# The front of a three-layer network: modulation sums by tile pairs and as row sums on VectorE, projections and block attention moved beside the recurrence

## The reference

```python
mod = (jax.nn.silu(c) @ w_ada[l] + b_ada[l])[:, None, :]        # 1024 -> 6144
sh1, sc1, gt1, sh2, sc2, gt2 = jnp.split(mod, 6, axis=-1)
xn = rms_norm(h, norm1_g[l]) * (1.0 + sc1) + sh1
proj = xn @ w_in[l]
qm, km, vm, zrw, gate_logits = jnp.split(proj, split_at, axis=-1)
qm = rope_partial(rms_norm(qm.reshape(B, S, 8, 64), q_norm_g[l]), positions)
km = rope_partial(rms_norm(km.reshape(B, S, 8, 64), k_norm_g[l]), positions)
o_moba = moba_attention(qm, km, vm)                             # causal, one block of 256
zrw = token_shift(zrw, rwkv_mu[l])
o_rwkv = rwkv7_time_mix(zr, zk, zv, zw, za, zg, ...)            # scan over 256 tokens, 8 heads of 64
g_moba, g_rwkv = jnp.split(jax.nn.sigmoid(gate_logits), 2, axis=-1)
mixed = g_moba * (o_moba @ w_proj_moba[l]) + g_rwkv * (o_rwkv @ w_proj_rwkv[l])
h = h + gt1 * (mixed @ w_out[l])
xn2 = rms_norm(h, norm2_g[l]) * (1.0 + sc2) + sh2
```

## Time and profile before

| | |
|---|---|
| median of 3 runs | 1921.0 us |
| the profiled execution | 1917.7 us, span 1915.9 us |
| PE busy | 1781.4 us (93%) |
| DVE, ACT, POOL busy | 1144.5, 793.8, 206.1 us |
| first matmul | at 16.09 us |
| first matmul of a projection | at 47.81 us |
| first matmul of `wq`, where the part that the change touches ends | at 437.83 us |
| PE busy before and after that point | 367.6 and 1413.8 us |

### The profile page before, as it was taken

One profiled execution on the slowest core, in us unless ns is written; L12 is line 12 of the kernel. 1 busy time (PEld: TensorE's weight loads), 2 busy tenths in 40 slices (PEclk: granted clock), 3 DMA queues, 4 the chain that ended last, 5 costly groups with the idle time before them and its releaser, 6 DMA issues.

```text
span 1915.9 us, 30068 instructions
## 1 busy us (share of the span) xinstructions
PE 1781.4 (93%) x13092; PEld 1631.8 (85%) x13092; DVE 1144.5 (60%) x1707; ACT 793.8 (41%) x1143; POOL 206.1 (11%) x84
## 2 busy tenths in 40 slices
PE   4979898888989899999999999999999998999987
PEld 2778787788989899998898888888899997988887
DVE  2373239555588748875435998555664546454654
ACT  3533323634434432234443222444434545544543
POOL 0030134200556620000000000000000000000000
PEclk8899999998999999999999999999999998999999
DMA  8223712243435443335453333555654343433320
GB/s 314 76 109 141 256 68 89 100 160 137 164 145 179 173 146 119 111 110 198 176 186 144 118 125 110 197 193 189 238 178 157 128 165 114 153 132 131 110 89 23
DMA packets 40022, 280.29 MB, mean 146 GB/s; under 512 B 4433, under 2 KB 4689, under 8 KB 7506
## 3 DMA queue, kind: packets, MB, share of 16 engines
q1 hardware_dynamic: 39024, 275.53, 40.4%
q10 hardware_dynamic: 866, 2.84, 0.4%
HBM read 277.30 MB, written 1.05 MB: 145 GB/s over the span
## 4 chain that ended last, share of the span: by engine, by line
PE 78%; DVE 13%; ACT 5%; POOL 2%; DMA 2%; issue 1%; ACTq 0%; DVEq 0%
PE ps L481 77%; DVE WL L1629 2%; POOL WL L2310 2%; ACT ar L1092 2%; DVE ar L1621 2%; ACT WH L1100 1%; DVE ar L1602 1%; DVE ar L2026 1%; DVE ar L2023 1%; DVE ar L1613 1%; DMA con<-in_con 1%; DVE ar L2030 1%; PE ps L609 0%; DVE ar L2042 0%; DMA ar<-in_in_qk 0%
## 5 line engine op out<-in xcount | busy, mean ns | idle before, releaser
L481 PE MATMUL ps<-RH,WH 128*128 128x256 f32 x2520 | 744.3, 295 | 52.8 <-DVE RL L1661 13.3
L481 PE MATMUL ps<-RL,WH 128*128 128x256 f32 x2520 | 722.8, 287 | 0.0
L481 PE MATMUL ps<-RH,WL 128*128 128x256 f32 x2520 | 721.9, 286 | 0.0
L1629 DVE TENSOR_TENSOR WL<-ar,WH 128x1024 fp32r<-128x1024 f32 (+1 forms) x398 | 468.2, 1208 | 374.2 <-ACT WH L1100 374.1
L1100 ACT ACTIVATE WH<-ar 128x1024 fp32r<-128x1024 f32 (+1 forms) x478 | 480.0, 1039 | 283.3 <-PE ps L481 269.1
L481 PEld LDWEIGHTS ps<-RH,WH 128*128 128x128 f32 x2520 | 493.8, 196 | 71.1 <-issue 21.5
L481 PEld LDWEIGHTS ps<-RL,WH 128*128 128x128 f32 x2520 | 494.2, 196 | 3.4 <-issue 2.9
L481 PEld LDWEIGHTS ps<-RH,WL 128*128 128x128 f32 x2520 | 493.3, 196 | 0.0
L481 PE MATMUL ps<-ar 128*128 128x64 f32 (+9 forms) x2988 | 339.4, 300 | 32.6 <-DMA con<-in_con 16.1
L481 PEld LDWEIGHTS ps<-ar 128*128 128x128 f32 (+6 forms) x2988 | 281.2, 172 | 71.2 <-issue 23.4
L481 PE MATMUL ps<-WH,RH 128*128 128x512 f32 (+1 forms) x704 | 261.8, 372 | 6.3 <-DVE RL L2004 6.3
(11 more groups left out here) (134 smaller groups left out, 979.9 us busy)
## 6 DMA issues: line engine op xcount, KB each, us to landing
ar<-in_u SPq DMA_DIRECT2D x64, 1024.0 KB, 4.8
ar<-in_v SPq DMA_DIRECT2D x64, 1024.0 KB, 4.7
ar<-in_ada SPq DMA_DIRECT2D x24, 1024.0 KB, 5.1
ar<-in_in_g SPq DMA_DIRECT2D x8, 1024.0 KB, 4.7
ar<-in_wq SPq DMA_DIRECT2D x8, 1024.0 KB, 4.8
ar<-in_a_qk SPq DMA_DIRECT2D x8, 1024.0 KB, 10.6
ar<-in_a_v SPq DMA_DIRECT2D x8, 1024.0 KB, 4.8
ar<-in_a_g SPq DMA_DIRECT2D x8, 1024.0 KB, 4.7
```

Of the source, the lines that this page charges most:

```text
L481: ins = q.matmul(o, l, r, start=start and i == 0, stop=stop and i == len(pairs) - 1, skip_group_check=skip)
L1629: q.tensor_tensor(l[:, x:z, :], src[:, x:z, :], h[:, x:z, :].bitcast(F32), ALU.subtract).then_inc(*v.up(("lo", n, i)))
```

## The change

It rewrites the order of the front and four of its parts.

1. **First modulation by tile pairs.** Chunk j of `ada` (j = 0 to 7) now holds scale and shift of feature tile j, and its sum follows its own product. DVE makes the two columns of `mod` for tile j, XM for it and, one tile later, the rest in RL; ACT makes RH tile by tile. Chunk 7 comes after the first half of `in_wag`. Of the constants only 134 columns (ones, selector, eps) are loaded at the start; the other 1664 and the small LoRA weights are issued by SP before the second `in_rkv` chunk. The rotary angles move behind the first projection.
2. **The other 4096 modulation sums as row sums.** Chunks `adr` hold 2 x 128 columns of `w_ada` transposed, 1024 long; c comes once more, as 128 equal rows (`cwide`), and DVE makes one sum by a `scalar_tensor_tensor` with `accum_out`, 32 in all, at places given by `DOTS`. PE, ACT and PSUM have no part in it.
3. **Projections.** `in_qk` stands beside the first solve (two units a step), the first half of `in_g` beside the second, the rest beside `states` (`UNITS`). The key norm and rotary steps stand beside the second solve (`queries`); the query norm is no longer applied to the queries but as a row factor of the scores (`q_rms`).
4. **Block attention** runs beside `states`, three sub-steps after each of its first 11 half steps (`HEADS`). The output norm of the recurrence is done by token halves; its second half stands beside `pm`, which now comes before `pr`. X is given up to the queries and keys and loaded again before `wo`.
5. The ring has six banks beside the recurrence, not five; the turns of v, al, be and kd and the bonus product move behind the start of `in_v`.

```diff
 WEIGHTS = {
-    "ada": (8, 2, 24), ...
+    "ada": (8, 2, 8), "adr": (2, 8, 16), ...
+DOTS = ((1, 1, 1, 1, 1, 1, 1, 1, 2, 2, 2, 2), (0, 0, 1, 1, 1, 1, 1, 1, 1, 1, 0, 0),
+        (0, 1, 0, 1, 0, 1, 0, 1, 0, 1, 0, 1, 0, 1, 0, 1))
+UNITS = ((2,) * 12, (1,) * 8 + (2,) * 4, (1, 0) * 5 + (1,) + (2,) * 5)
+HEADS = (3,) * 11 + (0,) * 5
...
@@ tensor_program: ada
-    def ada(j, more, of=ring):
+    def ada(j):
...
         ins.then_inc(*p.up(("ada", j)))
-        if more:
-            ada_sum(j - 1)
+        p.wait_ge(*on(("out", ("ada", j))))
+        b = bank(("ada sum", j))
+        for f in range(2):
+            ins = mm(b[:, f:f + 1], [(m.ada_rows[j % 2][:, f * P:(f + 1) * P], cst("sel"))])
+        ins.then_inc(*p.up(("ada sum", j)))
@@ tensor_program: front
-        for j in range(4):
-            ada(j, j > 0)
+        ada(0)
+        ada(1)
         colsum(("norm1",), m.XN, 8, "x squared")
-        for j in range(4, 8):
-            ada(j, True)
-        ada_sum(7)
+        for j in range(2, 7):
+            ada(j)
         zs = chain(proj_steps("in_wag", 0, by="xs"), proj_steps("in_rkv", 0, js=KRV))
-        some(zs, 8)
+        some(zs, 2)
+        ada(7)
+        some(zs, 6)
...
-        fill = beside_recurrence()
-        some(fill, 3)
         for hf in range(2):
-            for _ in pair(hf):
-                some(fill)
-        finish(fill)
-        more = proj_steps("in_qk", 0, of=side)
-        for _ in states():
-            some(more)
-        finish(more)
-        gates = proj_steps("in_g", 0, of=side)
-        for _ in norms():
-            some(gates, 4)
+            for i, _ in enumerate(pair(hf)):
+                some(dots, DOTS[hf][i])
+                some(fill, UNITS[hf][i])
+                if (hf, i) == (1, 0):
+                    q_sums()
+                    blksum("k norm", m.squares[1], ("qk squared", 1))
+                if hf == 1 and 5 <= i < 9:
+                    partners(2 * i - 10)
...
-        for i, _ in enumerate(at):
-            some(gates, i % 3 < 2)
+        for i, _ in enumerate(states()):
+            some(dots, DOTS[2][i])
+            some(fill, UNITS[2][i])
+            some(at, HEADS[i])
+            if i == 9:
+                y_sum("y mean", 0, m.Yy, ("out", ("y", 1)))
+            if i == 11:
+                y_sum("y var", 0, m.Ysq, ("y squared", 0))
+        steps = proj_steps("pm", 8, "oms")
+        some(steps, 2)
+        y_sum("y mean", 1, m.Yy, ("out", ("y", 3)))
+        some(steps, 5)
+        y_sum("y var", 1, m.Ysq, ("y squared", 1))
+        finish(steps)
         proj("pr", 12, "ors")
@@ vector_program
+    def dot_chunks():
+        for j in range(16):
+            feed.take()
+            ...
+            v.wait_ge(*m.loaded(c))
+            for f in range(2):
+                x, i = w[:, 1024 * f:1024 * f + 1024], 16 + 2 * j + f
+                v.wait_ge(*on("c wide silu"))
+                q.scalar_tensor_tensor(x, x, 1.0, m.cwide, ALU.mult, ALU.mult,
+                                       accum_out=mod[:, i:i + 1]).then_inc(*v.up(("adr", j)))
+                yield
@@ sync_program
+        if c == CHUNKS.index(("in_rkv", KRV[1])):
+            for dst, src in ((m.con[:, C1A:], m.D["con"][:, C1A:]), (m.lw[:, 0:512], m.D["w2a2"]), (m.lw[:, 512:1024], m.D["g2"]),
+                             (m.posi.bitcast(I32), m.D["pos"]), (m.w0[0:1, :], m.D["w0row"])):
+                q.dma_start(dst, src).then_inc(m.lora_loads, 16)
```

More of the change, by code:

```diff
@@ L43 @@
 WEIGHTS = {
-    "ada": (8, 2, 24), "in_wag": (8, 2, 1), "in_rkv": (8, 2, 6), "in_v": (8, 2, 2), "in_qk": (8, 2, 4),
+    "ada": (8, 2, 8), "adr": (2, 8, 16), "in_wag": (8, 2, 1), "in_rkv": (8, 2, 6), "in_v": (8, 2, 2), "in_qk": (8, 2, 4),
     "in_g": (8, 2, 8), "pm": (4, 4, 2), "pr": (4, 4, 2), "wo": (8, 2, 4), "wq": (8, 2, 8), "sub": (1, 16, 1),
@@ L50 @@
 }
-RAW = ("ada", "sub")
+RAW = ("ada", "adr", "sub")
 KRV = (2, 3, 0, 1, 4, 5)
@@ L877, in beside_recurrence @@
         yield from tok_steps("in_v", 0, of=side)
+        turn("v", m.zv, ("z", 12), side)
+        yield
         for nm, src in (("al", m.al), ("be", m.be), ("kd", m.kd)):
-            turn(nm, src, "al be", side)
+            turn(nm, src, "rwkv in", side)
             yield
-        for j in range(8, 24):
-            ada(j, j > 8, side)
+        yield from proj_steps("in_qk", 0, of=side)
+        yield from proj_steps("in_g", 0, of=side)
+    def dot_chunks():
+        for _ in range(16):
+            feed.take()
             yield
-        ada_sum(23)
+            yield
     def up(b_):
@@ L1203, in front @@
         AC(m.XN, m.X, ACT.Square, "x squared")
-        for j in range(4):
-            feed.take()
+        for j in range(2):
             ada_rows(j)
@@ L1299, in half_tanh @@
-        def half_tanh(t, f, n):
-            a.wait_ge(*on(t))
-            q.activation((m.Gm if f < 8 else m.Gr)[:, f % 8:f % 8 + n, :], pairs(tile(t)), ACT.Tanh,
-                         scale=0.5).then_inc(*a.up(("out", t)))
-        gates = walk("in_g", feed, half_tanh)
-        for _ in norms():
-            some(gates, 4)
+        a.wait_ge(*on("angle cos"))
+        AC(m.cA, m.cA, ACT.Sin, "rope ready")
+        a.wait_ge(m.c_load, 16)
+        AC(m.c_sigmoid, m.cwide, ACT.Sigmoid, "c wide sigmoid")
@@ new lines, in front @@
+        fill, dots = beside_recurrence(), dot_chunks()
+        some(fill, 4)
+        for hf in range(2):
+            for i, _ in enumerate(zip(group(2 * hf), group(2 * hf + 1))):
+                some(dots, DOTS[hf][i])
+                some(fill, UNITS[hf][i])
+                if (hf, i) == (0, 11):
+                    for k in range(4):
+                        AC(m.Aa[:, k, :], m.Aa[:, k, :], ACT.Identity, "bonus and shift", bias=vc("ln_b", k))
+                if (hf, i) == (1, 0):
+                    a.wait_ge(*on("q sums"))
+                    AC(m.q_rms, tile("q sums")[:, 0:16], ACT.Sqrt, ("out", "q sums"), bias=cst("eps", 3, 4))
+                    for f in range(2):
+                        t = ("k norm", f)
+                        a.wait_ge(*on(t))
+                        AC(half_of(m.k_root, 2 * f), tile(t), ACT.Sqrt, ("out", t), scale=1.0 / 64, bias=cst("eps", 0, 1))
@@ new lines, in queries @@
+    def queries(i):
+        if 2 <= i < 6:
+            k, r = m.qk[:, i + 2, :], m.k_root[:, i - 2, :]
+            v.wait_ge(*on(("out", ("k norm", 1))))
+            REC(r, r)
+            v.wait_ge(*on(("out", ("in_qk", 6))))
+            TT(k, k, r, ALU.mult, "k scaled")
+        if i == 2:
+            v.wait_ge(*on(("out", "q sums")))
+            REC(m.q_rms, m.q_rms)
+        if 6 <= i < 10:
+            f = 2 * i - 12
+            o, t = m.qk[:, f:f + 2, :], ("rotA", f)
+            r = m.rot[:, f % 4:f % 4 + 2, :]
+            v.wait_ge(*on("rope ready"))
+            v.wait_ge(*on(t))
+            TT(r, pairs(tile(t)), bc(m.sA, 2), ALU.mult, ("out", t))
+            TT(o, o, bc(m.cA, 2), ALU.mult)
+            TT(o, o, r, ALU.add, "qk ready")
@@ new lines, in scaled_scores, with y_centred, y_scaled @@
+    def scaled_scores(h, s, b):
+        for tt, (x, z) in enumerate(((0, 128), (128, 384))):
+            STT(s[:, x:z], b[:, x:z], m.q_rms[:, 8 * tt + h:8 * tt + h + 1], cst("mask3", x, z), ALU.mult, ALU.add)
+    def y_centred(hf):
+        y, t = m.Yy[:, :, hf * P:hf * P + P], ("y mean", hf)
+        v.wait_ge(*on(t))
+        STT(y, b4(tile(t)), -1.0 / 64, y, ALU.mult, ALU.add, ("y centred", hf))
+        v.mark(("out", t))
+    def y_scaled(hf):
+        ts = slice(hf * P, hf * P + P)
+        y, r = m.Yy[:, :, ts], m.Yrt[:, :, ts]
+        v.wait_ge(*on(("out", ("y var", hf))))
+        REC(r, r)
+        v.wait_ge(*v.last())
+        for k in range(4):
+            q.scalar_tensor_tensor(y[:, k, :], y[:, k, :], vc("ln_g", k), r[:, k, :], ALU.mult, ALU.mult).then_inc(*v.up())
+        v.wait_ge(*on("bonus and shift"))
+        TT(y, y, m.Aa[:, :, ts], ALU.add)
+        TT(y, y, m.Gg[:, :, ts], ALU.mult)
```

458 lines of the change are left out of this document (235 added, 223 removed).

## The result

The changed kernel takes 1963.9 us (median of 4 runs), the kernel before 1921.1 (4 runs): a ratio of 1.021, 95% interval 1.019 to 1.024. It is slower by 43 us; the forecast was 32 us faster. The first matmul of `wq` comes at 483.6 us in place of 437.8. From there on nothing has moved: 1478.8 us against the last row. So the loss lies in the front.

What follows compares the result with a forecast made beforehand. PE work was taken to bound the kernel, PE being busy for 93% of the span. Stages of 55.2 + 64.6 + 135.5 + 98.7 + 51.9 made a front of 405.9 against 437.8 us, so 1921.0 - 31.9 = 1889; range 1862 to 1912.

Steps and rivals of the forecast that it cites:

- rival D: Row sums on DVE: each takes two passes, 2.3 us in place of 1.23; 1905 us in all; chance 0.08.
- The second solve: Second solve: 28.8 us of solve, 23.0 of `in_g`, 7.8 of sums and rotary products, late first chunk 2.5; 62.3 us.
- the tail: `pr` to the end of the front: 51.9 us for 63.3 before, since `pm` has moved ahead; bounds 51 and 56.
- a sign that its terms are wrong: Front: PE busy for over 370 us would show the terms wrong; about 339 was expected.
- 1. Start, to the LoRA products: Start of the kernel to the LoRA products: 55.2 us for 60.8 before; bounds 50 and 62.
- the `ada` round of 2.4 us: Start: one `ada` chunk needs product, row copy 0.4, sum and signals, 2.4 us together.
- 2. To the first mask: LoRA products to the solve's first quads: 64.6 us for 68.1 before, bounds 59 and 70; first mask near 121.
- Rival B: DVE and POOL block each other: a full half lost for 12 chunks, 29 us; 1918, no change; chance 0.10.
- 3. The first solve: First solve: 58.9 us of PE work plus standstills of 6.2, 3.7, 1.2 and 3.2 us; 73.2 us.
- rival C: Three load slots: each of 12 weight chunks beside solves and states holds PE up 5.1 us; 1936; chance 0.10.
- 4. Solves to `pr`: End of the solves to `pr`: 98.7 us for 148.0 before, 75 to the last y, then 23.7; bounds 88 and 118.
- an unchanged idle time of 70: Front: PE work falls from 367.6 to about 339 us; with idle time unchanged the front takes 409 us.

Runs made afterwards that it cites:

- The filling: Changed kernel plus ten more 128 x 512 matmuls at the start, between an `ada` product and its sum: 1956.4 us.
- without the chunks: Changed kernel without its sixteen row-sum chunks, neither their loads nor their sums: 1927.2 us, ratio 1.0045.
- With the filling in place: Changed kernel plus two more 128 x 512 matmuls ahead of the three transposes of each head, 16 in all: 1949.9 us.
- short sums: Kernel before with `ada` chunks 8 to 23 as row-sum chunks on VectorE, each sum over 8 columns of 1024: 1900.4 us, ratio 0.989.
- the kernel with row sums alone: Kernel before with only `ada` chunks 8 to 23 made sixteen row-sum chunks on VectorE, at the same places: 1924.0 us, ratio 1.0015.

## Why the prediction was wrong

**Held.** A row sum in the changed kernel:

```profile
139.13 1.22 DVE L1945 SCALAR_TENSOR_TENSOR ar<-ar 128x1024 f32<-128x1024 f32 x1
140.27 0.08 DVE L1945 DVE_READ_ACCUMULATOR ar<-ar 128x1 f32 x1
```

It takes 1.22 us, what follows starts 1.15 us behind its start, and the read of the accumulator adds 0.08, so 1.24 was right and rival D false. The rule of the Trainium skill that stood behind rival D ("Vector Engine (DVE) Microarchitecture Reference", "Points that are easy to get wrong") does not hold here: the form takes 1.22 us with the accumulator and 1.23 without it. The second solve took 61.3 us for 62.3, the tail 53.0 for 51.9. The first PE instruction, at 8.8 for 7.5, was nearly right.

**The whole.** The front is 77.7 us over its forecast. Of this 39.5 are PE's busy time (378.5 for 339) and 38 its idle time (105 for 67). The prediction had named the first as a sign that its terms are wrong (over 370), and it gave slower than before a chance of 0.10.

**1. Start, to the LoRA products: forecast 55.2, measured 63.6.** The term that failed is the `ada` round of 2.4 us: 3.4 at the lower clock, for three chunks. I had it in the bounds ("with products and sums twice as long") and left it out of the value, though the trace of the kernel before has such products too:

```profile
35.56 1.93 PE L481 MATMUL ps<-ar 128*32 128x256 f32 x16
```

The filling brings the 2.4 us back. The column sum took 2.8 us more than forecast, 6.46, and with filling ahead of it is back at 3.70, though the windows give the granted clock as 1.00 around it (18 to 26 us). X landed 2.6 us late, at 13.7.

**2. To the first mask.** The stage took 72.5 us, I had 65.8. The four `rk` products stand beside POOL:

```profile
112.88 3.94 DVE L1828 SCALAR_TENSOR_TENSOR ar<-ar,vec 128x256 f32<-128x256 f32 x4
...
124.31 5.72 DVE L1838 SCALAR_TENSOR_TENSOR ar<-ar,vec 128x256 f32<-128x256 f32 x4
```

The last four take 5.72 us where four like them took 1.67 in the earlier trace rows. Rival B's mechanism is real, at some 4 us here and 6.3 with the four ahead of them; the 32 sums took 45.4 us in all, 1.43 each, where free of POOL they take 1.23. But the forecast had counted 4.7 us for POOL in this stage, so this explains under 2 of the 6.7 us. No run tried the rest apart, and its cause stays open.

**3. The first solve: forecast 73.2, measured 91.2.** I had priced a late load at 6.2, 3.7 and 1.2 us, walking through the steps as if a load only waited for its own slot. It waits for VectorE's sums, these wait behind the masks, and the masks wait for PE, which waits for the load: a ring, and each of its three turns costs the transfer, 7.0, 4.8 and 8.4 us. That is rival C, which I gave 0.10, in this solve alone: without the chunks it takes 65 us, 6.5 less for each of its four weight chunks, while the second solve was as forecast. "37 us of 59: enough room" is the sentence that failed: a share of busy time says nothing of an engine whose instructions stand one by one in a chain.

**4. Solves to `pr`: forecast 98.7, measured 142.6.** The largest miss, and all of it lies in the steps: up to the last y they took 120 us for 75, from there to `pr` 22 for 23.7. Middle steps of 11.5 us became 15.8 and 15.0. The steps' shape was right (PE and VectorE alternate) and its sizes came from rows at full clock. Beside states and attention there had been 23 us of `in_qk` and 46 of `in_g`; with 23 of `in_g` left there the clock falls, and I had kept the price of a matmul. With the filling in place a middle step takes 11.3, as forecast; but it shortens the stage by only 11 of the 43.9 us that this stage is over. Two steps that I had overlooked are longer still, 22.0 and 18.9 us (the additions stand at 352.29, 374.31 and 393.23):

```profile
361.92 9.61 PE ps L504 x54
...
371.97 1.06 ACT RH L1169
...
373.06 1.22 DVE RL L1699
374.31 0.76 DVE ar L2043 x2
...
378.34 4.75 DMA ar<-in_in_g
...
387.22 3.36 DVE ar L1675
...
393.23 0.77 DVE ar L2043 x2
```

In the first the split of attention's output (RH, RL) stands ahead of the addition. In the second a load of `in_g` that waited for a row sum stands in the chain, and then 8 us of the output norm of the first token half (from its root to its gate, the reciprocal at 387.22 among them). The forecast had this norm in no step. With filling the two steps take 20.1 and 18.9 us, without chunks 17.7 and 17.6, so clock and sums explain only a part of them. No run moved the split or the norm of the first half by itself.

**The sentence under all of it** was "with an unchanged idle time of 70 the front would take 409 us", and with it the price of nothing for the row sums. Taking the 27 us of work off PE was worth some 21 us in the kernel before (1900 us with short sums); the whole sums on VectorE cost 24 again.

## What to carry to other kernels

Before work is moved off the engine that is busiest, ask for each stage whether that engine or a chain through several engines sets its length, and price what is moved at the place where it lands: an instruction put between two links of a chain costs path time however idle its engine, here 0.7 us of its 1.24. Filling is worth something: a stage from which PE's side work is taken may run its remaining matmuls at the lower clock, so cost it at the durations of a slow stretch too. And where one queue issues loads in order into a few slots, each chunk that another engine releases late shortens the look-ahead of all that come behind it.

## What the hardware showed that was not expected

Sixteen matmuls whose results no one reads made a kernel faster by 14 us (11 in the front), and ten at the start by 7.5 (4 in the front). In the states the granted clock stood at 0.58 while PE was busy for 27 of 33 us and waited for VectorE in between, again and again. The Trainium skill ("TensorE: Matmul & The Clock Gate", "Loop structure matters more than you think") counts a copy by VectorE behind a matmul group among what does not break the warmth, where the next matmuls follow at once. Here the next group waits for VectorE's result, which that passage leaves open, and the lower clock is what the trace shows. The start also has two forms that no edit explains: the column sum took 3.70 us in the kernel before and 5.70 in the kernel with row sums alone, whose start is the same, and the first projection came at 47.8 and 51.2. The stretch behind `wq` has such forms too: the same instructions took 1472.2 to 1478.8 us. No run here says why.
